# Band attention by pairs of heads, and stick breaking scores bounded before a plain exponential

## The reference, cut to what matters

```python
z = jnp.einsum('bthd,bshd->bhts', q[:, lo:hi], k[:, :hi]) * scale
mask = ((lo + jnp.arange(SB_BLOCK))[:, None] > jnp.arange(hi)[None, :])
log_keep = jnp.where(mask, jax.nn.log_sigmoid(-z), 0.0)      # -softplus(z)
after = lax.cumsum(log_keep, axis=3, reverse=True) - log_keep
log_a = jnp.where(mask, jax.nn.log_sigmoid(z) + after, -jnp.inf)
a = jnp.exp(log_a); out = jnp.einsum('bhts,bshd->bthd', a, v[:, :hi])
```

```python
scores = jnp.einsum('bnqhd,bnkhd->bnhqk', qc, kb) * (B_HD ** -0.5)
scores = jnp.where(valid, scores + bias, -1e30)
probs = jax.nn.softmax(scores, axis=-1)
o = jnp.einsum('bnhqk,bnkhd->bnqhd', probs, vb)
```

## Time and profile before

| what | value |
|---|---|
| median of three runs | 1743.9 us |
| the profiled execution, its own time | 1743.94 us |
| its span, first to last instruction | 1742.0 us |
| TensorE busy | 1623.1 us (93%) |
| VectorE, ScalarE, GpSimd busy | 968.1, 744.0, 140.5 us |
| mean granted TensorE clock | 0.968 |
| chain that ended last | TensorE 80%, VectorE 9%, ScalarE 5% |
| HBM read over the span | 172.23 MB, 101 GB/s |

### The profile page before, as it was taken

One profiled execution on the slowest core, in us unless ns is written; L12 is line 12 of the kernel. 1 busy time (PEld: TensorE's weight loads), 2 busy tenths in 40 slices (PEclk: granted clock), 3 DMA queues, 4 the chain that ended last, 5 costly groups with the idle time before them and its releaser, 6 DMA issues.

```text
span 1742.0 us, 19733 instructions
## 1 busy us (share of the span) xinstructions
PE 1623.1 (93%) x7990; PEld 1267.6 (73%) x7990; DVE 968.1 (56%) x1257; ACT 744.0 (43%) x1049; POOL 140.5 (8%) x97
## 2 busy tenths in 40 slices
PE   6999999899899898887999999999898999999998
PEld 3787777668698554565888876667676888888877
DVE  4669879796845888746246335553335333332344
ACT  4456656553424778644212454422323222231242
POOL 0000000132100000043000000000121000000120
PEclk7999999999999999998999999989999999999999
DMA  7344433333752110111221212212121222223243
GB/s 306 133 135 160 142 121 121 109 116 127 274 209 75 46 49 25 49 64 51 82 73 49 73 60 68 67 49 74 71 97 64 97 96 98 97 87 115 85 148 118
DMA packets 47450, 177.76 MB, mean 102 GB/s; under 512 B 3680, under 2 KB 20320, under 8 KB 31744
## 3 DMA queue, kind: packets, MB, share of 16 engines
q1 hardware_dynamic: 30432, 167.44, 26.5%
q10 hardware_dynamic: 16928, 9.06, 1.9%
HBM read 172.23 MB, written 4.26 MB: 101 GB/s over the span
## 4 chain that ended last, share of the span: by engine, by line
PE 80%; DVE 9%; ACT 5%; issue 3%; POOL 1%; DMA 1%; POOLq 0%; SPq 0%; DVEq 0%; ACTq 0%
PE bank L620 21%; PE bank L622 20%; PE bank L621 20%; PE bank L652 2%; PE bank L650 2%; PE bank L651 2%; PE zz L873 2%; PE zz L940 1%; PE bank L955 1%; DVE wlo L1090 1%; DVE W L1377 1%; ACT whi L1680 1%; POOL HL L2204 1%; DMA A<-astream 1%; PE tt L736 1%
## 5 line engine op out<-in xcount | busy, mean ns | idle before, releaser
L620 PE MATMUL bank<-HH,whi 128*128 128x512 f32 x1480 | 615.6, 416 | 58.3 <-issue 18.2
L622 PE MATMUL bank<-HH,wlo 128*128 128x512 f32 x1480 | 587.8, 397 | 0.0
L621 PE MATMUL bank<-HL,whi 128*128 128x512 f32 x1480 | 587.2, 397 | 0.0
L620 PEld LDWEIGHTS bank<-HH,whi 128*128 128x128 f32 x1480 | 284.2, 192 | 157.9 <-issue 93.0
L622 PEld LDWEIGHTS bank<-HH,wlo 128*128 128x128 f32 x1480 | 283.8, 192 | 62.5
L621 PEld LDWEIGHTS bank<-HL,whi 128*128 128x128 f32 x1480 | 284.9, 192 | 54.2 <-issue 3.1
L1090 DVE TENSOR_TENSOR wlo<-raw,whi 128x2048 fp32r<-128x2048 f32 (+2 forms) x118 | 267.4, 2266 | 99.0 <-ACT whi L1680 96.6
L1680 ACT ACTIVATE whi<-raw 128x2048 fp32r<-128x2048 f32 (+2 forms) x118 | 222.3, 1884 | 99.6 <-PE bank L622 98.7
L650 PE MATMUL bank<-whi,HH 128*128 128x256 f32 x256 | 74.0, 289 | 0.0
L651 PE MATMUL bank<-whi,HL 128*128 128x256 f32 x256 | 72.4, 283 | 0.0
L652 PE MATMUL bank<-wlo,HH 128*128 128x256 f32 x256 | 72.4, 283 | 0.0
(11 more groups left out here) (289 smaller groups left out, 2140.8 us busy)
## 6 DMA issues: line engine op xcount, KB each, us to landing
raw<-wstream SPq DMA_DIRECT2D x113, 1024.0 KB, 4.8
aslot<-tstream SPq DMA_DIRECT2D x24, 512.0 KB, 3.3
A<-astream SPq DMA_DIRECT2D x8, 1024.0 KB, 18.1
AC<-scratch ACTq DMA_DIRECT2D x16, 512.0 KB, 5.8
QT<-tstream SPq DMA_DIRECT2D x12, 512.0 KB, 5.3
OZ<-tstream SPq DMA_DIRECT2D x12, 512.0 KB, 7.2
raw<-wstream SPq DMA_DIRECT2D x4, 768.0 KB, 5.0
X<-xT SPq DMA_DIRECT2D x1, 2048.0 KB, 8.1
```

The lines of the kernel that those rows point to most:

```text
L620: e.matmul(o, wh[:, k, c], hi[:, kb0 + k, :], start=first and k == 0, stop=False)
L621: e.matmul(o, wh[:, k, c], lo[:, kb0 + k, :], start=False, stop=False)
L622: x = e.matmul(o, wl[:, k, c], hi[:, kb0 + k, :], start=False, stop=last and k == kb - 1)
```

## The change

Stick breaking: the copy of the scores (L1368) becomes one instruction that takes the minimum with 40 and adds the mask. On ScalarE, Abs and Exp of the negative are replaced by one Exp of the score itself, then Ln(1 + x) as before; the VectorE pass that added max(score, 0) is gone. What is computed is the softplus of min(score, 40). A masked score is -1e30, whose exponential is 0.

Band attention: a unit is a pair of heads and one query block, 16 units, laid out as stick breaking has it: two score products one after the other into `zz`, one scale-and-bias, one maximum, one negation and one reciprocal for both heads, the exponentials still one for each head, the scaling by a broadcast tensor product in place of one with a scalar for each row, transposes of both heads into `tt`, one copy, value products with the heads alternating. The buffers `zz`, `tt` and `PT` are single, the third score buffer is SR. Rounds have three steps, 20 rounds, woven 60 to 92; branch blocks now yield after each k-step, so that the other generator has 64 + 32 = 96 steps. The bias is loaded for two heads at a time (four loads of 512 KB).

The diff, cut to TensorE, VectorE, ScalarE and the loads:

```diff
-    BW = [sbt(f"BW{i}", [128, S], F32, ph2) for i in range(2)]
-    PS = [sbt(f"PS{i}", [128, S], F32, ph2) for i in range(3)]
-    PT = [sbt(f"PT{i}", [128, 4, 128], F32, ph2) for i in range(2)]
+    BW = [sbt(f"BW{i}", [128, 2, S], F32, ph3) for i in range(2)]
+    PS = [sbt(f"PS{i}", [128, 2, S], F32, ph3) for i in range(2)] + [SR]
+    PT = sbt("PT", [128, 2, S], F32, ph3)
...
+    some = lambda a: [a] if 0 <= a < 16 else []
... SyncE
-                e.dma_start(BW[h % 2][:, :], rbx[h]).then_inc(l_bw[h % 2], 16)
+                e.dma_start(BW[n % 2][:, :, :], rbx[2 * n:2 * n + 2].rearrange("h p j -> p h j")).then_inc(l_bw[n % 2], 16)
... TensorE
+        def band():
+            for r in range(-1, 19):
+                for a in some(r - 2):
+                    w.wait_ge(s_bp, a + 1)
+                    w.wait_ge(s_bt2, a)
+                    for j in range(2):
+                        for b in range(a % 4 + 1):
+                            c = slice(128 * b, 128 * b + 128)
+                            x = e.transpose(tt[:, j, c], PS[a % 3][:, j, c], ident)
+                    x.then_inc(s_btr, 1)
+                yield
+                for a in some(r - 3):
...
+                    w.wait_ge(s_bt2, a + 1)
...
+                    for b in range(tb + 1):
+                        for j in range(2):
+                            h = 2 * n + j
+                            x = e.matmul(aux[4][64 * j:64 * j + 64, 128 * tb:128 * tb + 128], VB[:, b, 64 * h:64 * h + 64],
+                                         PT[:, j, 128 * b:128 * b + 128], start=(b == 0), stop=(b == tb))
+                    x.then_inc(s_bv, 1)
+                yield
+                for a in some(r + 1):
...
+                    w.wait_ge(s_bs, a)
+                    for j in range(2):
+                        o = 64 * j
+                        x = e.matmul(zz[:, j, 0:hi], QB[o:o + 64, n, 128 * tb:hi], KB[o:o + 64, n, 0:hi],
+                                     start=True, stop=True)
+                    x.then_inc(s_bq, 1)
+                yield
...
-                run(blocks(chunk_of["wa", n], [("wa", n)], (n % 4,), 512, oa_ready, OA[:, 0, :, :], OA[:, 1, :, :]))
-                yield
-        weave((pipelined([band_unit(a) for a in range(32)], 4), 36), (chain(gates_a(), branch_a()), 96))
+                yield from blocks(chunk_of["wa", n], [("wa", n)], (n % 4,), 512, oa_ready, OA[:, 0, :, :], OA[:, 1, :, :])
+                yield
+        weave((band(), 60), (chain(gates_a(), branch_a()), 92))
... VectorE, stick breaking
-                    e.tensor_tensor(att_z(a, hi), zz[:, :, 0:hi], bmask[:, S - hi:S].unsqueeze(1).to_broadcast([128, 2, hi]),
-                                    ALU.add).then_inc(s_zc, 1)
+                    e.scalar_tensor_tensor(att_z(a, hi), zz[:, :, 0:hi], 40.0,
+                                           bmask[:, S - hi:S].unsqueeze(1).to_broadcast([128, 2, hi]),
+                                           ALU.min, ALU.add).then_inc(s_zc, 1)
...
-                    own(e.scalar_tensor_tensor(av, att_z(a, hi), 0.0, av, ALU.max, ALU.add))
... VectorE, band
+                    e.scalar_tensor_tensor(av, zz[:, :, 0:hi], 0.125, BW[n % 2][:, :, S - hi:S], ALU.mult, ALU.add).then_inc(s_bs, 1)
+                    own(e.tensor_reduce(m[:, 0:2], av, AX, ALU.max))
+                    e.tensor_scalar(m[:, 2:4], m[:, 0:2], -1.0, None, ALU.mult).then_inc(s_bm, 1)
+                yield
...
+                for a in some(r - 1):
+                    own(e.reciprocal(m[:, 6:8], m[:, 4:6]))
+                    e.tensor_tensor(av, av, m[:, 6:8].unsqueeze(2).to_broadcast([128, 2, hi]), ALU.mult).then_inc(s_bp, 1)
+                yield
... ScalarE, stick breaking
-                    own(e.activation(av, att_z(a, hi), ACT.Abs))
-                    own(e.activation(av, av, ACT.Exp, scale=-1.0))
+                    own(e.activation(av, att_z(a, hi), ACT.Exp))
                     e.activation(av, av, ACT.Ln, bias=1.0).then_inc(s_ex, 1)
... ScalarE, band
+                for a in some(r):
+                    for j in range(2):
+                        x = e.activation(av[:, j, :], av[:, j, :], ACT.Exp, bias=m[:, 2 + j:3 + j], accum_out=m[:, 4 + j:5 + j])
+                    x.then_inc(s_be, 1)
+                yield
+                for a in some(r - 2):
+                    e.activation(PT[:, :, 0:hi], tt[:, :, 0:hi], ACT.Copy).then_inc(s_bt2, 1)
+                yield
```

More of the change, by code:

```diff
@@ L279, in program @@
     ph2 = ExitStack()
[L280 to L282 removed]
     OB = sbt("OB", [128, 2, 4, S], F32R, ph2)
     SGA = sbt("SGA", [128, 8, S], F32, ph2)
[L285 to L286 removed]
+    sm = [sbt(f"sm{i}", [128, 8], F32, ph2) for i in range(2)]
+    ph3 = ExitStack()
+    BW = [sbt(f"BW{i}", [128, 2, S], F32, ph3) for i in range(2)]
+    PS = [sbt(f"PS{i}", [128, 2, S], F32, ph3) for i in range(2)] + [SR]
+    PT = sbt("PT", [128, 2, S], F32, ph3)
+    ph3.close()
+    ph3 = ExitStack()
+    SGB = sbt("SGB", [128, 4, S], F32, ph3)
+    ph3.close()
     ph2.close()
@@ L550, in branch_a @@
                     behind("wa", n)
-                yield
-        weave((pipelined([band_unit(h, tb) for h in range(8) for tb in range(4)], 4), 36),
-              (chain(gates_a(), branch_a()), 96))
+                yield from idle(4)
+        weave((band(), 60), (chain(gates_a(), branch_a()), 92))
         for i2 in range(2):
@@ L931, in _, with band @@
         weave((hgrn(), 70), (in2_rest(), 115))
[L934 to L957, removed]
+        def band():
+            for r in range(-1, 19):
+                for a in some(r - 2):
[8 more added lines that the diff above has]
+                for a in some(r - 3):
+                    n, tb = divmod(a, 4)
+                    w.wait_ge(s_bt2, a + 1)
+                    w.wait_ge(s_vb, 4)
+                    if tb == 0:
+                        w.wait_ge(s_bo, n)
+                    for b in range(tb + 1):
[6 more added lines that the diff above has]
+                for a in some(r + 1):
+                    n, tb = divmod(a, 4)
+                    hi = 128 * (tb + 1)
+                    w.wait_ge(s_qn, 8)
+                    w.wait_ge(s_or, 4)
+                    w.wait_ge(s_bs, a)
[5 more added lines that the diff above has]
+                yield
@@ L1576, in branch_a @@
             for n in range(8):
+                yield from idle(3)
                 branch(n)
@@ L1580, in branch_a @@
                 yield
-        weave((pipelined([band_unit(a) for a in range(32)], 4), 36), (branch_a(), 96))
+        weave((band(), 60), (branch_a(), 92))
         band_low(3)
@@ L2247, in _, with load_bias, band @@
             low("in2", k, T[k % 3][:, :])
-        def load_bias(h):
-            if h < 8:
-                w.wait_ge(l_bw[h % 2], 16 * (h // 2 + 1))
-                e.memset(BW[h % 2][0:64, 448:512], -1e30).then_inc(s_bw, 1)
-        def band_unit(h, tb):
-            if tb == 0:
-                if h == 0:
-                    load_bias(0)
-                load_bias(h + 1)
-            yield
-            yield
-            yield
+        def load_bias(n):
+            if n < 4:
+                w.wait_ge(l_bw[n % 2], 16 * (n // 2 + 1))
+                e.memset(BW[n % 2][0:64, :, 448:512], -1e30).then_inc(s_bw, 1)
+        def band():
+            for r in range(-1, 19):
+                if r % 4 == 0 or r < 0:
+                    load_bias((r + 4) // 4)
+                yield from idle(3)
         def gates_a():
```

89 lines of the change are left out of this document (40 added, 49 removed).

## The result

The changed kernel takes 1693.6 us (median of four runs, 1693.2 to 1698.0) against 1743.4 us (four runs, 1740.82 to 1748.07): 49.8 us less. The ratio is 0.9717, with a 95% interval of 0.9691 to 0.9744, that is 45 to 54 us. The forecast was 1699 us, range 1684 to 1719. The profiled execution of the changed kernel took 1698.0 us, with a span of 1696.1: 4 us above its median, which matters when spans are compared.

What follows compares the result with a forecast made beforehand. TensorE, busy 93% of the span, was taken as the bound: its own work in the band, its waits and slow clock in stick breaking. 1744 - 31 (band) - 14 (stick breaking) = 1699 us, range 1684 to 1719.

Steps and rivals of the forecast that it cites:

- Stick breaking, 14 us forecast: Stick breaking: fewer TensorE waits and less slow clock, TensorE's work unchanged; gain 14 us, bounds 8 and 24.
- where I had 2.4: Stick breaking's slow clock: of 5.4 us lost behind three long stretches, 3 stay.
- one Abs less ahead of each wait: Stick breaking, ScalarE's queue ahead of the copy TensorE waits for: takes at least 0.73 us from each wait.
- The band, 31 us forecast: Band attention: pairing heads and dense work to the end start the gb blocks near 1149 us; gain 31 us.
- The length built from them at full clock, 105.8 us: Band stage: 16 units of 2.42 us (38.7) plus 288 dense products (67.1), 105.8 us at full clock.
- waits and slow clock: Band stage, added to 105.8 us: 2 for slow clock at the start, 2 for bias, 4 for steady waits.
- The bias was late as foreseen: Band start: first scale-and-bias waits for a load twice as large; 2 us taken, bounds 0 and 3.
- the 8.3 us of slow clock at the end of the old stage: Old band's last 17 us without dense work, clock at 0.51: 17 x 0.49 = 8.3 us lost.
- (a): Rival, band: copies out of PSUM become the bound, waits 22 us in place of 6; 1715 us, chance 0.08.
- (b): Rival, stick breaking: tables, casts and tanh lockstep set the waits; gain 4 us, not 14; 1709 us, chance 0.08.
- (c): Rival, band: the two heads' products don't overlap, scores and values cost 26 us more; 1725 us, chance 0.03.
- (d): Rival, band: single buffers make TensorE wait for each pair's whole chain; slower, 1763 us, chance 0.02.

Runs made afterwards that it cites:

- the cover added alone: Kernel before, with branch blocks giving way after each k-step so dense steps last as long as the band, units still single heads: 1733.5 us, ratio 0.9955.
- the kernel with both heads in the same place: Changed kernel, band scores of both heads from the same 64 partitions, values head by head into the same 64 columns: 1710.2 us, ratio 0.9828.
- the kernel without cover: Changed kernel with branch blocks again issued whole in one step, so the band's last fifth has no dense work beside it: 1700.4 us, ratio 0.9782.
- the kernel with gates first: Changed kernel with seven more gate k-steps ahead of the band, the rest woven 60 to 86: 1681.8 us, ratio 0.9662.

## Why the prediction was right, point by point

**The bound.** TensorE's own time in the band and waits in stick breaking were the right reading. Each part alone confirmed the sizes: the stages gave 14 and 33 us separately.

**Stick breaking, 14 us forecast, 14.1 measured.** Idle time fell by 9.6 us where I had 12 (21.0 to 11.4, not to 9), and the rest, 4.5 us, is slow clock and the like, where I had 2.4. That the sum met the measurement within 0.1 us is luck; the reason behind it was half right. I had argued from ScalarE's queue, with VectorE as company. The runs show the VectorE pass worth as much as Abs, and either one enough to lose most of the gain. The step that I argued from, one Abs less ahead of each wait, gives 4.6 us by itself and not 14, as the kernel with the VectorE pass back shows. The trace of before held the sign, and the prediction does not use it: a wait is put down to the engine that came last, and what that engine had waited for itself is one step further back. In 558 to 740 us:

```profile
ACT W L1935 <- DVE W L1385: 23.8, 11, 5.0
```

ScalarE's exponential, which stands ahead of the copy, had waited 23.8 us for VectorE.

**The band, 31 us forecast, 35.5 measured.** TensorE's groups came out as halved from stick breaking: 13.1, 12.3 and 11.5 us for 13.3, 12.9 and 12.0. The length built from them at full clock, 105.8 us, stands against 112.0 - 4.9 idle - 1.7 slow clock = 105.4. The forecast put the end 116.0 us behind the last token product (1149.1 less 1033.1), and it was 112.0. The mis-sized terms are small: I started the stage at the first scores and so kept the 2.0 us of idle time ahead of them, which the new weave fills with dense steps, since it issues the scores in its third step; and waits and slow clock were 6.6 us in place of 8. The bias was late as foreseen and cost 3.0 us of waiting where I took 2. One size in the prediction was off without entering the sum: the 8.3 us of slow clock at the end of the old stage count all 17 us, but TensorE was busy for 15.1 of them. With the cover added alone, its busy time in the stage fell by 5.7 us (139.8 to 134.1) and its idle time by 3.4.

**The rivals.** (a) Copies out of PSUM as the bound of the band: no, 4.9 us idle in all, of which 3.0 at the start. What the Trainium skill says may happen to packed products (TensorEngine Tiling (Array Packing), PSUM Bottleneck), that copying out of PSUM comes to limit them, isn't seen here, with VectorE busy 65.5 and ScalarE 52.9 of 112.0 us. (b) Waits set by tables: a third of what stayed, not what went. (c) No overlap: the kernel with both heads in the same place shows that case, 129.3 us, and the changed kernel isn't it. (d) A serial chain: seen only in the kernel without cover, in the tail, where the stage is 8.3 us longer.

**The clock.** With one pass put back, 5.6 of 10.4 us lost and 3.9 of 9.5 were idle time, and the rest went with the lower clock. The forecast's size was right at the band's start (2 us, measured 1.7) and behind its end (the stretch at 0.53 is gone), and too small in stick breaking, where it took 2.4 us and up to 4.5 came.

What stays open: the medians of the kernel with gates first and of the changed one differ by more than their stages (ratios 0.9662 and 0.9717, stages 5.7 us). The intervals leave room for it (0.9632 to 0.9692 and 0.9691 to 0.9744), and in the two profiled executions, whose spans differ by 11.5 us, 4.5 of them lie ahead of the first scores and 1.5 behind the band, in code that neither changes. Why these parts vary between executions no run shows.

## What to carry to other kernels

Products with a contraction of 64 or an output of 64 columns should be issued in pairs that lie in different partitions or columns, as direct neighbours; here that took them from 22.1 and 20.9 us to 13.1 and 12.3 at an unchanged number of instructions, and it can be read from a stage that already does it. Keep dense steps beside a latency chain to its very end, and some ahead of its first load, since a bare stretch costs its waits and then the slow clock behind them. Before crediting a wait to the engine that the profile names, look up what that engine waited for itself, and then put the removed work back on each engine in turn: here a pass on either of two engines was enough to lose most of the gain.

## What the runs showed of the hardware

The overlap of products in different columns doesn't need strict alternation in short runs: eight value products took 1.03 us alternating, 1.52 in turn (six products' time) and 1.90 in the same columns. This fits about two products overlapping on each side of the seam.

Scores of two heads from the same 64 partitions took 1.91 us for 512 keys, from different ones 1.06, although the records in the trace have nearly the same mean (466 and 485 ns): the gain shows in the start of the next instruction and in the group's busy time, not in the duration of one.
